# Gated linear attention inside a two-block transformer kernel: level products issued in pairs that share PSUM banks, one step moved, and the gates' products in another PSUM ring

## The reference, cut to what matters

```
g = log_sigmoid(g_lr @ w_gate + b_gate) / 16          # 4 heads, key width 128
b = cumsum(g)                                          # over the rows
decay[t, s] = exp(b[t] - b[s])          for s <= t
scores[t, s] = sum_k q[t, k] * k[s, k] * decay[t, s, k]
out = scores @ v        (then a norm per head, a gate, and an output projection)
```

## Time and profile before

| | |
|---|---|
| time, median of 3 | 1425.56 us (1425.4 to 1426.72) |
| the profiled execution's own time | 1424.74 us |
| its span | 1422.8 us |
| mean granted TensorE clock | 0.999 |
| TensorE busy | 1405.9 us, 99% |
| VectorE busy | 942.7 us, 66% |
| ScalarE busy | 723.5 us, 51% |
| GpSimd busy | 160.8 us, 11% |

### The profile page before, as it was taken

The page is one execution under the profiler, slowest core; times in us unless marked ns, Lnnn a source line. Parts: engine busy times, 40 slices in busy tenths (PEclk is TensorE's granted clock), DMA queues, the critical chain, the costliest instruction groups (busy, mean ns, idle before and its releaser), DMA issues.

```text
span 1422.8 us, 19077 instructions
## 1 busy us (share of the span) xinstructions
PE 1405.9 (99%) x7339; PEld 1148.8 (81%) x7339; DVE 942.7 (66%) x1290; ACT 723.5 (51%) x1042; POOL 160.8 (11%) x237
## 2 busy tenths in 40 slices
PE   9999999999999999999999999999999999999997
PEld 7888888688888888888878888887877788788886
DVE  6666567886675667665796857755568566765553
ACT  6444355664544444444755645446556644654442
POOL 1700010010000000000181100001552110100000
PEclk9999999999999999999999999999999999999999
DMA  9686765156876777777534688773945355565551
GB/s 312 201 251 204 255 209 198 67 188 199 250 252 208 229 242 240 249 241 242 200 126 157 216 197 259 246 221 112 252 148 193 119 176 178 163 207 183 201 194 59
DMA packets 236346, 286.15 MB, mean 201 GB/s; under 512 B 37028, under 2 KB 160592, under 8 KB 236256
## 3 DMA queue, kind: packets, MB, share of 16 engines
q1 hardware_dynamic: 235856, 284.56, 62.8%
q10 hardware_dynamic: 400, 0.38, 0.1%
HBM read 280.70 MB, written 4.20 MB: 200 GB/s over the span
## 4 chain that ended last, share of the span: by engine, by line
PE 92%; DVE 4%; ACT 1%; issue 1%; POOL 1%; DMA 1%; SPq 0%; POOLq 0%; ACTq 0%; DVEq 0%
PE ps L582 29%; PE ps L585 28%; PE ps L583 28%; DVE wlo L474 1%; PE pst L937 1%; PE pst L778 1%; PE pst L1213 1%; ACT whi L465 1%; DMA raw<-in_ffn_w_in_dram 1%; PE ps L1160 0%; PE ps L555 0%; PE pst L1526 0%; ACT junk L715 0%; PE ps L1197 0%; PE ps L1675 0%
## 5 line engine op out<-in xcount | busy, mean ns | idle before, releaser
L474 DVE TENSOR_TENSOR wlo<-raw,whi 128x1024 fp32r<-128x1024 f32 (+2 forms) x474 | 564.1, 1223 | 252.5 <-ACT whi L465 252.1
L465 ACT ACTIVATE whi<-raw 128x1024 fp32r<-128x1024 f32 (+2 forms) x474 | 472.3, 1040 | 241.0 <-PE ps L585 93.8
L582 PE MATMUL ps<-whi,xh 128*128 128x512 f32 (+2 forms) x1438 | 564.9, 393 | 2.3 <-DVE wlo L474 1.3
L583 PE MATMUL ps<-wlo,xh 128*128 128x512 f32 (+2 forms) x1438 | 553.6, 385 | 0.0
L585 PE MATMUL ps<-whi,xl 128*128 128x512 f32 (+2 forms) x1438 | 545.2, 385 | 0.0
L582 PEld LDWEIGHTS ps<-whi,xh 128*128 128x128 f32 x1438 | 270.0, 188 | 62.5 <-issue 4.0
L585 PEld LDWEIGHTS ps<-whi,xl 128*128 128x128 f32 x1438 | 269.9, 188 | 55.0
L583 PEld LDWEIGHTS ps<-wlo,xh 128*128 128x128 f32 x1438 | 270.2, 188 | 51.0
L582 PE MATMUL ps<-whi,gh 128*128 128x512 f32 x440 | 172.0, 391 | 0.0
L583 PE MATMUL ps<-wlo,gh 128*128 128x512 f32 x440 | 171.2, 389 | 0.0
L585 PE MATMUL ps<-whi,gl 128*128 128x512 f32 x440 | 153.4, 389 | 0.0
(11 more groups left out here) (267 smaller groups left out, 906.3 us busy)
## 6 DMA issues: line engine op xcount, KB each, us to landing
raw<-in_ffn_w_in_dram SPq DMA_DIRECT2D x174, 512.0 KB, 5.4
raw<-in_ffn_w_out_dram SPq DMA_DIRECT2D x40, 1024.0 KB, 5.8
raw<-in_w_in_dram SPq DMA_DIRECT2D x26, 1024.0 KB, 5.0
adat<-in_w_ada_dram SPq DMA_DIRECT2D x96, 256.0 KB, 3.1
raw<-in_w_ffn_gate_dram SPq DMA_DIRECT2D x22, 512.0 KB, 4.2
raw<-in_w_ffn_up_dram SPq DMA_DIRECT2D x22, 512.0 KB, 5.2
raw<-in_hyb_w_in_dram SPq DMA_DIRECT2D x10, 1024.0 KB, 5.2
raw<-in_gla_w_in_dram SPq DMA_DIRECT2D x10, 1024.0 KB, 5.2
```

The costliest lines, as they stand in the source:

```text
L465: e.activation(split_of(whi, j), raw_of(j), ACT.Copy).then_inc(*whi_made.up(j))
L474: e.tensor_tensor(split_of(wlo, j), raw_of(j), split_of(whi, j).bitcast(F32), ALU.subtract).then_inc(*wlo_made.up(j))
L582: e.matmul(ps[:, 0:n], a, whi_of(j, k), start=first and k == 0, stop=False)
L583: last = e.matmul(ps[:, 0:n], a, wlo_of(j, k), start=False, stop=False)
```

## The change

The products of levels 0 to 7 are issued two levels at a time at the step of the odd one. The pairs (0,1), (2,3) and (4,5) share one `tb` bank, the odd level in its second half; levels 6 and 7 keep a bank each. VectorE puts both levels of a pair at that step too. `(0,0)` is gone from subunit 3. One more blank step stands ahead of level 4's. The gates' products go into the ring `acc` instead of `tb`. The steps with the change:

```diff
-            GLA += ["-"] * {6: 1, 7: 2}.get(n, 0)
+            GLA += ["-"] * {3: 1, 6: 1, 7: 2}.get(n, 0)
...
-                return [["k", (1, "a")], [(2, "a")], ["q", (1, "e"), (3, "a")], [(0, 0), (2, "e"), (1, "m")]][i]
+                return [["k", (1, "a")], [(2, "a")], ["q", (1, "e"), (3, "a")], [(2, "e"), (1, "m")]][i]
...
             n, j = s
             if j != 0:
                 return
-            X = gX[n % 4]
-            ps = tb.next(("lv", n), (lv_put, n))
-            for done in tb.freed:
-                e.wait_ge(*done)
-            if n == 0:
-                e.wait_ge(*gla_qk.at("gq", 2))
-            else:
-                e.wait_ge(*(lv_kd if n % 2 else lv_k).at(n))
-                e.wait_ge(*lv_q.at(n))
...
+            if n % 2 == 0:
+                return
+
+            for n in (n - 1, n):
+                if n % 2 == 0 or n == 7:
+                    tb.next(("lv", n), (lv_put, n if n >= 6 else n + 1))
+                    for done in tb.freed:
+                        e.wait_ge(*done)
+                ps = lv_bank(n)
+                if n == 0:
+                    e.wait_ge(*gla_qk.at("gq", 2))
+                else:
+                    e.wait_ge(*(lv_kd if n % 2 else lv_k).at(n))
+                    e.wait_ge(*lv_q.at(n))
...
+        def lv_bank(n):
+            if n >= 6:
+                return tb.of("lv", n)
+            return tb.of("lv", n - n % 2)[:, n % 2 * 256:(n % 2 + 1) * 256]
...
                 if n == 1:
                     e.wait_ge(*gla_qk.at("gk", 2))
+                    e.wait_ge(*gla_qk.at("gq", 2))
...
-                e.wait_ge(*lv_dot.at(n))
...
+            if j != 0 or n % 2 == 0:
+                return
+            for n in (n - 1, n):
+                ps = lv_bank(n)
+                e.wait_ge(*lv_dot.at(n if n >= 6 else n | 1))
...
         def pe_gate_dot(e, hp):
-            ps = tb.next(("gate", hp), (gate_min, 2 * hp + 1))
-            for done in tb.freed:
+            ps = acc.next(("gate", hp), (gate_min, 2 * hp + 1))
+            for done in acc.freed:
                 e.wait_ge(*done)
```

More of the change, by code:

```diff
@@ L1508, in pe_gla_step @@
                 return
-            X = gX[n % 4]
-            ps = tb.next(("lv", n), (lv_put, n))
-            for done in tb.freed:
-                e.wait_ge(*done)
-            if n == 0:
-                e.wait_ge(*gla_qk.at("gq", 2))
-            else:
-                e.wait_ge(*(lv_kd if n % 2 else lv_k).at(n))
-                e.wait_ge(*lv_q.at(n))
-            if n == 8:
+            if n == 8:
+                ps, X = tb.next(("lv", 8), (lv_put, 8)), gX[0]
+                for done in tb.freed:
+                    e.wait_ge(*done)
+                e.wait_ge(*lv_k.at(8))
+                e.wait_ge(*lv_q.at(8))
                 for i in range(4):
@@ L1521, in pe_gla_step @@
                                  start=i == 0, stop=True, skip_group_check=True)
-            else:
-                lh, rh = (gKT, gQT) if n == 0 else (X, X)
+                t.then_inc(*lv_dot.up(8))
+                return
[4 more added lines that the diff above has]
+                    tb.next(("lv", n), (lv_put, n if n >= 6 else n + 1))
+                    for done in tb.freed:
+                        e.wait_ge(*done)
+                ps = lv_bank(n)
[4 more added lines that the diff above has]
+                    e.wait_ge(*lv_q.at(n))
+                lh, rh = (gKT, gQT) if n == 0 else (gX[n % 4], gX[n % 4])
                 for i in range(8):
@@ L1526, in pe_gla_step @@
                         t = e.matmul(ps[k:k + 32, i * width:(i + 1) * width], lh[:, i * P + k:i * P + k + 32],
-                                     rh[:, i * P + q:i * P + q + width], start=i == 0, stop=True, skip_group_check=True)
-            t.then_inc(*lv_dot.up(n))
+                                     rh[:, i * P + q:i * P + q + width], start=i == 0 and (n >= 6 or n % 2 == 0),
+                                     stop=True, skip_group_check=True)
+                t.then_inc(*lv_dot.up(n))
+        def lv_bank(n):
+            if n >= 6:
+                return tb.of("lv", n)
+            return tb.of("lv", n - n % 2)[:, n % 2 * 256:(n % 2 + 1) * 256]
         def dve_gla_step(e, s):
@@ L1557, in dve_gla_step @@
                                 ALU.mult).then_inc(*lv_q.up(n))
-            if j == 0:
-                ps = tb.of("lv", n)
-                e.wait_ge(*lv_dot.at(n))
-                if n == 8:
-                    e.tensor_copy(gOFF[:, :], ps[:, :]).then_inc(*lv_put.up(n))
-                    return
+            if j == 0 and n == 8:
+                e.wait_ge(*lv_dot.at(8))
+                e.tensor_copy(gOFF[:, :], tb.of("lv", 8)[:, :]).then_inc(*lv_put.up(8))
+                return
+            if j != 0 or n % 2 == 0:
+                return
+            for n in (n - 1, n):
+                ps = lv_bank(n)
+                e.wait_ge(*lv_dot.at(n if n >= 6 else n | 1))
                 if n < 6:
@@ L1571, in dve_gla_step @@
                           .to_broadcast([P, 8, 32]))
[L1572 to L1575, removed]
+                    e.copy_predicated(by_8(gC[:, :]), mk, by_8(ps)).then_inc(*lv_put.up(n))
+                elif n == 6:
+                    e.wait_ge(*s_cleared.at())
                     e.tensor_copy(by_8(gS[0:32, :])[:, :, 32:64], by_8(ps[0:32, 0:256]))
@@ L1768, in act_gates @@
                     hd = 2 * hp + j
-                    e.activation(E1[:, hd * 256:(hd + 1) * 256], tb.of("gate", hp)[:, j * 256:(j + 1) * 256],
+                    e.activation(E1[:, hd * 256:(hd + 1) * 256], acc.of("gate", hp)[:, j * 256:(j + 1) * 256],
                                  ACT.Abs, bias=vector("bg", hd)).then_inc(*gate_abs.up(hd))
@@ L1784, in dve_gates @@
                     hd = 2 * hp + j
-                    e.tensor_scalar(G[:, hd * 256:(hd + 1) * 256], tb.of("gate", hp)[:, j * 256:(j + 1) * 256],
+                    e.tensor_scalar(G[:, hd * 256:(hd + 1) * 256], acc.of("gate", hp)[:, j * 256:(j + 1) * 256],
                                     vector("bg", hd), 0.0, ALU.add, ALU.min).then_inc(*gate_min.up(hd))
```

## The result

The changed kernel took 1427.52 us (median of 15 runs, 1426.29 to 1429.76) against 1425.50 us of the kernel before (15 runs, 1423.66 to 1427.85) beside it: a ratio of 1.0017, 95% interval 1.0010 to 1.0024. The forecast was 1424.8 us. It is about 2 us slower, where 0.8 us faster was forecast. The profiled execution is among its slow ones (1429.55 us, span 1427.8 us); why is told at the end of the experiments.

The account below looks back on a forecast made before the run. TensorE, busy 1405.9 of 1422.8 us, was taken as the bound, with VectorE setting level 3. Level 3 -0.35, pairs -0.56, level 8 +0.15 make -0.76 us on 1424.74; with that execution 0.82 under the median, 1424.8 us, range 1423.0 to 1427.1.

Parts of the forecast that it names:

- the case that was taken as the likeliest: TensorE before level 3: wait grows from 2.3 to some 3.6 us, level 3 comes 0.35 us earlier; chance 0.60.
- the second rival: TensorE behind the longer wait before level 3: clock falls to 1.2 GHz, losing 2.3 us, time 1427.1; chance 0.14.
- The pair (4,5): TensorE behind level 3: issuing levels 4 and 5 together saves 0.28 us in full.
- It fits, with 0.2 us or more to spare: Level 4's products to level 7's multiplication: 5.8 to 6.8 us, within TensorE's 7.0 us of other work.
- Level 8: TensorE's level 8 needs level 6's bank, free about 754.7, asked for at 754.5: 0.15 us charged, bounds 0 and 0.5.
- the gates' 0.95 us: TensorE before k's transposes: the stall on the gates' `tb` banks goes, 0.95 us.
- level 0 at 722.5: TensorE reaches subunit 5, where levels 0 and 1 are now issued, about 2.15 us earlier, at 722.5.
- the hold of GpSimd: GpSimd's first step for level 4 must await level 0's products, so it is held 2.25 us.
- (4,"a"): GpSimd's first step for level 4: at 3.1 us level 3 is 0.85 us earlier, at 4.0 us 0.05 later.
- the chain behind it: From the end of GpSimd's first level 4 step to VectorE's last multiplication for level 3: 6.9 us.
- The third rival: Nothing is gained: GpSimd's delay reaches later levels, or level 7 waits 0.5 us; 1425.5 to 1426.3, chance 0.18.
- What GpSimd's rest is worth to VectorE: VectorE before level 3 runs faster while GpSimd rests before 722.5; at the range's end level 3 gains 0.65 us.

Follow-up runs that it names:

- a5: Changed kernel with pairs only for levels 0 to 3, levels 4 to 7 issued singly and the extra blank step out; ratio to the kernel before 1.0001.
- a1: Changed kernel with 20 unread 128x128 products of ones added on TensorE between levels 2 and 3; ratio to the kernel before 1.0004.
- a4: Changed kernel with 12 unread 128x128 products of ones added on TensorE between levels 2 and 3; ratio to the kernel before 0.9996.
- a6: Changed kernel with levels 4 to 7 issued singly, the extra blank step out, and 12 unread products of ones between levels 2 and 3; ratio to before 0.9987.
- b1: Kernel before with only the gates' products moved to the `acc` ring; ratio to the kernel before 1.0001.
- a2: Changed kernel with GpSimd's first step for level 4 no longer waiting for level 0's products; ratio to the kernel before 1.0024.
- c2: Changed kernel with TensorE alone issuing the pair (2,3) at subunit 8 instead of 7; ratio to the kernel before 1.0014.
- a0: The changed kernel itself run once more, unaltered; ratio to the kernel before 1.0012.

## Why the prediction was wrong

Two steps failed, each by about as much. Between the forecast's -0.76 us and the stage's +2.33 lie 1.59 us of clock and 1.71 us in levels 4 to 8 (-0.41 taken, +1.30 measured), less 0.23 us for level 3. Either alone would have turned the forecast gain into a loss of about 0.6 us.

- **The first failed step** is the case that was taken as the likeliest: that the wait before level 3 only grows, to "some 3.6 us", and costs nothing by it. It grew to 3.44 us, level 3 was ready 0.58 us sooner (0.35 taken), and then the clock fell. This stood there as the second rival, with a chance of 0.14 and a price of 2.3 us; it cost 1.59 here and 2.54 in a5's profile. a1, a4 and a6 show it: with the wait filled, the 1.6 us return. The Trainium skill, "TensorE: Matmul & The Clock Gate", section "What's actually happening", has the clock fall with idleness, and the trace agrees with 0.50 behind 3.44 us and 1.00 behind 2.26.
- **The second failed step** is the chain behind level 3. The pair (4,5) saved 0.30 us (0.28 taken). But "It fits, with 0.2 us or more to spare" was wrong: I followed the chain through ScalarE, 5.8 to 6.8 us, and not VectorE's own list behind its held copy, 7.5 us, in which both puts and level 6's multiplication had moved and most of it ran beside GpSimd. The wait was 0.83 us.
- **Level 8**, the other half of this second step, was charged 0.15 us and cost 0.90. The put of level 6 stood behind a `wlo` that was late itself: ScalarE had waited 1.70 us for level 5's put before its table load and its splits, which I hadn't carried on from there. With the level 7 wait and both pairs' savings, this part is 1.25 us slower than single levels (a4 against a6), where 0.41 us faster was forecast.
- **Right:** the gates' 0.95 us, level 0 at 722.5 (721.86, with 0.64 us of drift ahead of the stage) and the hold of GpSimd (2.25 us forecast and measured) came as worked out, and the gates' gain turned into waiting (b1: +0.08 us). (4,"a") took 3.64 us, between the 3.1 and 4.0 taken, and the chain behind it 6.5 us instead of 6.9. The third rival's wait before level 7 (0.5 us taken, 0.83 measured) came as well, on top of the second.
- What GpSimd's rest is worth to VectorE was argued and left at the end of the range. By a2 it is the reason that level 3 gained anything: without that rest level 3 came at 30.71 us, as before the change (30.70).

## What to carry to other kernels

Getting an engine sooner to a wait that another engine ends was not free on TensorE (2.26 us of waiting became 3.44, and 1.59 us were lost behind it): look at how long the wait becomes, and move other work into it or leave the engine late. When steps are merged, follow each engine's own list behind the instruction that now waits, not only the chain of data; here the puts that moved by one step cost more than the merged bursts saved. And a cheap place to win is an engine that asks too early: moving two steps on TensorE alone gave 0.9986, as good as any kernel here, and about 1.2 us by the stage.

## What the runs showed of the hardware

- In the level stage the grant was 0.50 behind waits of 3.40 to 3.88 us in each of four profiles, and 1.00 behind 2.20, 2.26, 2.33 (c2, before level 7) and 2.95 us. It is no clean line: in the changed kernel's first profile the wait of 2.37 us at 1019 us was followed by a grant of 0.50 too. In a2 and a5 it fell within the wait, 2.4 to 2.5 us after TensorE had gone idle; in the changed kernel's first profile it fell 1.5 us after TensorE had begun again, in a0 as it began. The low level lasted about 3.5 us in the changed kernel and over 6 us in a2 and a5. What decides between these cases, no run here shows.
- 24 records of products of ones (12 products), 128x128 in fp32, took 2.94 us and were enough to hold the clock at 1.00 through the same gap in both profiles that have them (a4, a6).
- The products of a second level issued right behind those of another cost 0.60 us (1.505 for the two) against 0.90 alone.
- Three VectorE operations with two SBUF operands took 5.74 us beside a busy GpSimd and 2.57 us without it.
